# A projection-heavy two-block layer on one core: thirty short self-waits of TensorE taken out, three longer ones put in

## The reference, cut to what matters

```
h = rmsnorm(x, ln_g);  proj = h @ w_in              # 52 blocks of 128 columns
... gated MLP, gated delta rule, cross attention
x = x + mixed @ w_out                               # 16 blocks
h = rms_norm(x, ...); proj = h @ w_in_2             # 80 blocks
... stick-breaking attention, forgetting attention
merged = sig(g_a) * (o_a @ w_a) + sig(g_b) * (o_b @ w_b);  x = x + merged @ w_out_2
q = h @ w_query; scores per head; top 16 pairs of keys -> expert ids, gates
act = gelu(h . expert_u[id]);  x += (gate * act) . expert_v[id]
x = rms_norm(x, final)
```

## Time and profile before

| what | value |
|---|---|
| median of 3 runs | 2993.87 us (2992.84 to 2997.76) |
| span of the profiled execution, first to last instruction | 2964.4 us |
| the profiled execution's own time | not recorded; the median less the span is 29.5 us |
| TensorE matmuls busy | 2882.6 us (97%), 24232 of them |
| GpSimd / ScalarE / VectorE busy | 2269.0 / 1308.1 / 1060.5 us |
| chain that ended last | 80% TensorE, 9% issue, 5% VectorE, 4% GpSimd |

### The profile page before, as it was taken

How to read it: one execution, slowest core, us unless ns; L and a number is a source line. 1 busy time by engine, 2 the same in 40 slices (tenths; PEclk the granted TensorE clock), 3 DMA queues, 4 the chain that set the end, 5 groups by cost and what they waited for, 6 DMA issues and landing times.

```text
span 2964.4 us, 58621 instructions
## 1 busy us (share of the span) xinstructions
PE 2882.6 (97%) x24232; PEld 2839.9 (96%) x24232; DVE 1060.5 (36%) x1544; ACT 1308.1 (44%) x1551; POOL 2269.0 (77%) x925
## 2 busy tenths in 40 slices
PE   7999988999999999999998999999999999999998
PEld 7999978899998999999998999999999999999998
DVE  6103356345121342224598871402104040133322
ACT  6364362554442444444454664343433434343333
POOL 6777740289774788988785568888998888899986
PEclk9999999999998999999999999999999999999999
DMA  6544420155543455555454565465565655655653
GB/s 244 171 158 172 157 88 13 45 184 198 171 159 113 142 178 196 198 193 185 157 198 170 223 232 209 173 227 184 194 229 176 224 184 194 218 209 195 216 187 113
DMA packets 85703, 524.37 MB, mean 177 GB/s; under 512 B 8657, under 2 KB 23121, under 8 KB 24402
## 3 DMA queue, kind: packets, MB, share of 16 engines
q1 hardware_dynamic: 68258, 489.12, 46.8%
q10 hardware_dynamic: 17328, 33.56, 3.0%
HBM read 503.77 MB, written 18.87 MB: 176 GB/s over the span
## 4 chain that ended last, share of the span: by engine, by line
PE 80%; issue 9%; DVE 5%; POOL 4%; ACT 0%; POOLq 0%; DVEq 0%; ACTq 0%
PE banks L1411 80%; POOL wlo L405 4%; DVE rest L1268 1%; PE banks L1520 0%; DVE i L1267 0%; DVE i L1270 0%; DVE v L1266 0%; DVE v L1269 0%; DVE cand L1307 0%; DVE cand L1308 0%; DVE picks L1309 0%; DVE T L829 0%; DVE ti L1270 0%; DVE ti L1267 0%; ACT kd L612 0%
## 5 line engine op out<-in xcount | busy, mean ns | idle before, releaser
L405 POOL TENSOR_TENSOR wlo<-raw,whi 128x1024 fp32r<-128x1024 f32 x920 | 2264.4, 2481 | 645.2 <-ACT whi L428 643.9
L428 ACT ACTIVATE whi<-raw 128x1024 fp32r<-128x1024 f32 x920 | 948.3, 1056 | 788.6 <-PE banks L1411 779.5
L1411 PE MATMUL banks<-xhi,whi 128*128 128x256 f32 x4672 | 644.3, 281 | 13.2 <-ACT whi L428 6.1
L1411 PE MATMUL banks<-xlo,whi 128*128 128x256 f32 x4672 | 642.6, 280 | 0.0
L1411 PE MATMUL banks<-xhi,wlo 128*128 128x256 f32 x4672 | 636.8, 279 | 1.9 <-POOL wlo L405 1.9
L1411 PEld LDWEIGHTS banks<-xhi,whi 128*128 128x128 f32 x4672 | 586.6, 190 | 17.0 <-issue 9.5
L1411 PEld LDWEIGHTS banks<-xlo,whi 128*128 128x128 f32 x4672 | 587.6, 190 | 2.7
L1411 PEld LDWEIGHTS banks<-xhi,wlo 128*128 128x128 f32 x4672 | 583.9, 189 | 2.6 <-POOL wlo L405 2.5
L897 DVE TENSOR_TENSOR X<-banks,X 128x256 f32 (+1 forms) x112 | 47.4, 424 | 747.8 <-PE banks L1411 747.8
L1411 PE MATMUL banks<-hid_lower,whi 128*128 128x256 f32 x2048 | 280.3, 279 | 0.0
L1411 PEld LDWEIGHTS banks<-hid_lower,whi 128*128 128x128 f32 x2048 | 256.3, 189 | 1.2
(11 more groups left out here) (368 smaller groups left out, 2368.8 us busy)
## 6 DMA issues: line engine op xcount, KB each, us to landing
raw<-in_w_exp SPq DMA_DIRECT2D x256, 1024.0 KB, 4.8
raw<-in_w_in SPq DMA_DIRECT2D x132, 1024.0 KB, 4.8
raw<-in_w_out SPq DMA_DIRECT2D x32, 1024.0 KB, 4.8
raw<-in_w_br SPq DMA_DIRECT2D x16, 1024.0 KB, 4.8
raw<-in_w_q SPq DMA_DIRECT2D x16, 1024.0 KB, 4.8
gates<-gst ACTq DMA_DIRECT2D x16, 1024.0 KB, 4.8
gch<-gates ACTq DMA_DIRECT2D x7, 2048.0 KB, 12.5
raw<-in_w_kv SPq DMA_DIRECT2D x8, 1024.0 KB, 9.4
```

The costliest lines, as they stand in the source:

```text
L405: pool.tensor_tensor(wlo[:, s, :, :], raw[:, j, h * HALF:(h + 1) * HALF, :], whi[:, s, :, :].bitcast(F32), ALU.subtract).then_inc(lo_ready, 1)
L428: act.activation(whi[:, (2 * j + h) % 4, :, :], raw[:, j, h * HALF:(h + 1) * HALF, :], ACT.Copy).then_inc(hi_ready, 1)
L1411: return nc.tensor.matmul(o, lhsT, rhs, start=start, stop=stop, **k)
```

## The change

The pauses, their semaphore `beat` and the parameter `paused` are gone. A unit may get `emptied=(semaphore, value)`: its first matmul then waits for that too. Three units get one, each on a semaphore that TensorE's own last matmul ahead of it raises, so that TensorE has nothing in flight when it goes on: unit U_IN2 + 55 (behind the last `weighted_values`), the first unit of up0 (behind the key scores), and the first unit of down0 (behind the last half unit of up2). No matmul is added, dropped or moved.

```diff
-            def pause(k, z):
-                if k == HALF - 1:
-                    z.then_inc(beat, 1)
-                    beats[0] += 1
-                elif k == 0:
-                    pe.wait_ge(beat, beats[0])
-
-            def unit_body(u, j, hi, lo, par, paired=False, fresh=None, between=None, paused=False):
+            def unit_body(u, j, hi, lo, par, paired=False, fresh=None, between=None, emptied=None):
...
                     pe.wait_ge(evac[j % 2], par)
+                if emptied is not None:
+                    pe.wait_ge(*emptied)
...
-                        z = mm(oo, whi[:, s0 + h, k, :], hi[:, tile(k), :], start=opens and k == 0, stop=False)
-                        if paused and h == 0 and k == HALF - 1:
-                            pause(k, z)
+                        mm(oo, whi[:, s0 + h, k, :], hi[:, tile(k), :], start=opens and k == 0, stop=False)
...
-                            if paused and h == 0 and k == 0:
-                                pause(k, z)
...
-            units(55, 56)
+            unit(U_IN2 + 55, emptied=(sg("wv_mm"), 4))
             segment(U_IN2 + 56, 24)
...
-                    segment(u0, KT, fresh=split(L_EXP) if e == 0 else None)
+                    segment(u0, KT, fresh=split(L_EXP) if e == 0 else None, emptied=(sg("key_scores"), 8) if e == 0 else None)
                 elif e < EXPERT_CHUNKS - 1:
-                    segment(u0, KT, False, *gated(e), gates_of(e))
+                    segment(u0, KT, False, *gated(e), gates_of(e), emptied=(pe_half, 2 * u0) if e == 0 else None)
```

More of the change, by code:

```diff
@@ L304, in program @@
         lin_src, lin_hi, lin_lo, lin_lo2 = sem("lin_src"), sem("lin_hi"), sem("lin_lo"), sem("lin_lo2")
-        conv_used, beat = sem("conv_used"), sem("beat")
+        conv_used = sem("conv_used")
         signals = {}
@@ L1411, in mm @@
                 return nc.tensor.matmul(o, lhsT, rhs, start=start, stop=stop, **k)
-            beats = [0]
-            def pause(k, z):
-                if k == HALF - 1:
-                    z.then_inc(beat, 1)
-                    beats[0] += 1
-                elif k == 0:
-                    pe.wait_ge(beat, beats[0])
-            def unit_body(u, j, hi, lo, par, paired=False, fresh=None, between=None, paused=False):
+            def unit_body(u, j, hi, lo, par, paired=False, fresh=None, between=None, emptied=None):
                 s0 = (2 * j) % 4
@@ L1485, in gates_of, with unit, segment @@
                 return lambda q: ((sg("hid_lo"), 4 * e + q + 1),) * 2
-            def unit(u, hi=xhi, lo=xlo, fresh=None, between=None):
-                unit_body(u - u % 2, u % 2, hi, lo, u // 2, False, fresh, between)
-            def segment(u0, n, paired=False, hi=xhi, lo=xlo, fresh=None, between=None):
+            def unit(u, hi=xhi, lo=xlo, fresh=None, between=None, emptied=None):
+                unit_body(u - u % 2, u % 2, hi, lo, u // 2, False, fresh, between, emptied)
+            def segment(u0, n, paired=False, hi=xhi, lo=xlo, fresh=None, between=None, emptied=None):
                 for j in range(2):
-                    unit_body(u0, j, hi, lo, u0 // 2, paired, fresh if j == 0 or paired else None, between if j == 0 else None, j == 1)
+                    unit_body(u0, j, hi, lo, u0 // 2, paired, fresh if j == 0 or paired else None, between if j == 0 else None,
+                              emptied if j == 0 else None)
                 with pe.Fori(1, n // 2) as i:
```

## The result

The changed kernel takes 2983.76 us, median of 8 runs (2976.99 to 2992.47); the kernel before, beside it, 2998.66 us (2992.84 to 3001.76). The ratio is 0.996, interval 0.9948 to 0.9972: faster by 0.4%, 15 us, where 33 us from a base of 2993.87 were forecast.

A forecast was written before the change was run, and what follows sets the result against it. TensorE, 97% busy, was taken to bound the kernel. Head +0.5, middle -3.6, U_Q -0.2 and tail -29.6 us sum to -32.9; with span 2964.4 plus 29.5 this gave 2961 us, range 2956 to 3006.

The forecast's parts named there:

- Two paces, 113 and 117.5 ns, that last until TensorE runs dry: In TensorE's matmul stream: each restart draws one pace anew, 4.5 ns or 4% apart, which then holds.
- the median less the span is 29.5 us: Base of the sum: 29.5 us added to the traced span of 2964.4 us to reach timed runs.
- the tail: Segments down0 to down7, 9984 matmuls: all fast once pauses go, forecast at -29.6 us.
- the middle: Unit 55 to U_OUT2, about 2730 matmuls: -3.6 us if the restart is fast, +8.7 if slow.
- I take it to come out fast again: Ahead of down0: the tail's first draw was fast in the trace and expected fast again, its code being unchanged.
- The gating stalls: Up3 to up7: late GpSimd subtractions stall TensorE five times, each a new draw costing 0.1 to 0.2 us.
- rival A: Slow pace drawn at down0 or up3's first gating stall holds to the end: 3001 to 3018 us, chance 0.26.
- Unit 55: Restart behind the added wait: wait costs 0.2 us; middle -3.6 us if drawn fast, +8.7 if slow.
- Down0's and up0's added waits at 0: Ahead of down0 and up0: added waits cost nothing, as TensorE stands still for VectorE there or later anyway.
- the search wait as a cover: Inside up1: TensorE's 11.41 us wait for `picks` absorbs whatever up0 gains or loses, so 0.
- Pauses at 0.2 us each, 6 us in all: Removing 29 pauses (up0's left out) saves 0.21 us each, 6 us, besides any draw of pace.
- If runs of the changed kernel lie 20 us apart, each run draws for itself: Sign that the prediction is wrong as a whole: a spread of 20 us between runs of the changed kernel.

The follow-up runs named there:

- e5: The changed kernel again, unaltered: 2986.91 us; the kernel before beside it 2996.39 us, ratio 0.997.
- e1: The kernel before, unchanged, profiled once more: 2937.47 us, with nine runs beside it at 2930.3 to 2939.33 us.
- e8: The kernel before, unchanged, profiled a third time: 2932.76 us.
- e7: Against the kernel before: its kind of self-wait in every second unit of all segments, 190 instead of 30; 3030.9 us, before beside it 2996.39.
- e16: The kernel of e7 again, on a chip where before took 2998.22 us: 3031.03 us.
- e2: The changed kernel without its three added waits, so no pauses either: 2979.61 us, ratio 1.0161 to the kernel before.
- e13: The changed kernel again, on another chip: median 2966.85 us (2943.8 to 2995.0), ratio 1.0067 to the kernel before.
- e3: The changed kernel without its three waits, with 104 self-waits of five kinds in every second unit of segments down0 to down7: 2987.3 us.
- e14: The kernel of e11 again, beside a kernel before at 2998.22 us: 3034.14 us.
- e11: The kernel of e7 plus one unread float32 128x128 matmul ahead of the first unit of each pair: 2999.79 us.
- e4: The changed kernel without its three waits, with unread transposes or float32 matmuls ahead of every second unit of segments down0 to down7: 3034.06 us.

## Why the prediction was wrong, step by step

- **Two paces, 113 and 117.5 ns, that last until TensorE runs dry:** right. The traces show them and no third; 8914 matmuls in one piece in the changed kernel's, 9964 in e5's. The turn always lay at a wait, a stall or a change of the kind of matmul.
- **The failed step: "the median less the span is 29.5 us", and the draws of one trace taken for the kernel's.** 2.2 us lie around the span. The other 27 us were the difference between the traced execution and the timed ones. The trace had 5 fast segments of 13. An execution of before at 2934 us has all 13 (e1, e8). None near 2998 was traced; that it has next to none is worked out: e7 and e16, on two chips where before is near 2998, have self-waits that leave slow, and 13 x 768 x 4.4 ns = 44 us for the tail and 2730 x 4.4 ns = 12 us for the middle make up most of the 64 us between the two. So the 27.6 us that were to be saved in the tail were counted from a state that the timed runs weren't in, and the sum's sign could be read from it as little as its size. The three timed runs, 5 us apart, were a hint: 13 independent draws of 3.4 us each would likely have spread more, and 29.5 us of surroundings had no row.
- **The terms of the sum, trace against trace:** the tail, forecast at -29.6 us, came at +11.2, since the stall in up3 drew slow; the middle, forecast at -3.6, at +8.7, since unit 55 drew slow. Together -32.9 forecast and +16.9 measured. With the prediction's own base this outcome would have been 2964.4 + 16.9 + 29.5 = 3010.8 us. That the time came at 2983.8, only 23 us off and inside the range, is luck: 50 us of wrong draws against 27 us of wrong base.
- **"I take it to come out fast again" (the tail's start):** right in the trace, and in e2 and e13; wrong in e5. So it too is a draw.
- **The gating stalls:** forecast as new draws, right: in up3, at 1917, and slow. That was the middle of rival A, +10.5 us forecast for the tail; trace against trace it was +11.2. The stall cost 0.37 us (481 ns from load to load instead of 113), more than the 0.1 to 0.2 that were put down. All three traces of the changed kernel have a slow tail from up3 on or earlier; whether 0.26 was too low a chance three traces can hardly tell. The chances don't add up either: "slower 0.28" is more than the 0.26 of A, the only rival that is clearly slower. The one fast outcome I relied on the earlier trace rows was one of an execution with other draws.
- **Unit 55:** slow instead of fast, +8.7 forecast for that side, +8.7 measured up to the key scores. e2 shows that the added wait isn't needed for it: without it the unit was slow too.
- **Down0's and up0's added waits at 0, the search wait as a cover:** right. Down0's stall is 2.87 us on both sides. Up0 was slow in e5 and e13, and the time from the key scores to `picks` didn't grow by its 4.9 us (143.5 us in both, 144.3 in the changed kernel's first trace); the wait for `picks` shrank from 11.40 to 5.72 us.
- **Pauses at 0.2 us each, 6 us in all:** right by the trace (329 against 113 ns from load to load). With the tail's fast start (1060 matmuls at 4.4 ns, 4.7 us) this would make 11 of the 15 us that the change gained over before near 2998. That is an estimate: no execution of before near 2998 was traced, and the other 4 us weren't placed.
- **"If runs of the changed kernel lie 20 us apart, each run draws for itself":** they lie 15 us apart (8 runs), then 13 (12 runs), then 51 (e13). So the sign came up, in e13.

What the change does, then, is to take away the 30 places at which TensorE starts over, in nearly every execution in one way throughout (the first trace is the exception). Where before is near 2998 us this gains 0.3 to 0.4% (two measurements); where it is near 2934 it loses, by 1.6% in e2's measurement, whose kernel lacks the three waits as well, and by 0.7% in e13's (interval 0.1 to 1.2%, on the chip where both kernels fell into groups). What makes an execution of the one kind or the other, and so decides where the phase doesn't, stays open. It isn't the program alone (before shows both on one chip), nor the chip alone (two of the seven measurements had both kinds on one chip, the other five one kind only), nor the clock, which is granted at 0.98 of full in both.

## What to carry to other kernels

Before a sum is made on a trace, put its span plus what lies around it (2.2 us here, read off a run that lists both) beside the timed runs: if they don't meet, the trace shows another execution than the timing, and its stalls and paces are one draw. Count instructions in windows of equal length where an engine is "97% busy": a 4% difference in pace is invisible on the page. A self-wait on TensorE costs 0.2 us at once and may cost 3.4 us per 768 matmuls after it; measure such a change on several chips, or its sign is that of the chip. Where two runs of the same code differ, look at the single gaps just ahead of the place where they part: part of the answer here stood in a pattern of 2 ns.

## What the runs showed of the hardware

- A stream of 128x256 fp32r matmuls, each with new weights, runs at 113.3 or 117.8 ns each at full clock, for as long as nothing interrupts it (1043 and 8913 gaps in the changed kernel's trace).
- At the fast pace the gaps are 113 and 114 ns with a mean of 113.33, 340 ns for three (2722 gaps in e3, behind unit 55); at the slow pace three gaps of about 119, 117.5 and 116.7 ns repeat, 353.3 ns in all.
- Which pace follows a self-wait goes with 0.7 to 1.0 ns in its mean length, and repeats within most executions: 160 of 160 self-waits that were entered fast left slow in e14, 178 of 178 left fast in e11.
- A single float32 matmul 128x128 in a slow stream turns it fast at one of the three phases of the slow pattern (162 of 162) and never at the other two (0 of 97).
- Short runs of other matmuls set the pace too, without a wait: in e4 twelve 128x128 transposes left fast eight times of eight, eight or sixteen left slow seven times of eight each.
- GpSimd's subtraction of 128x1024 takes 2.39 to 2.42 us with no VectorE arithmetic beside it (222 in the changed kernel's tail) and up to 3.40 beside VectorE's gating. The seven ahead of 1917.45 took 3.19 on average, over TensorE's 2.72 us per half unit at the fast pace, and TensorE stalled. VectorE's multiplication suffers as well: 1.22 us at 1888.80, 3.41 at 1896.10.
